# Placing and loading the modulation tiles of a two-layer transformer chain between its dense weight tiles

## The reference, cut to what matters

```
cond_lat = jax.nn.silu(c)
cond_ctx = jax.nn.silu(c_ctx)
for i in range(DEPTH):
    mod = (cond_lat @ ada_w[i] + ada_b[i])[:, None, :]
    modc = (cond_ctx @ ada_w[i] + ada_b[i])[None, None, :]
    sh1, sc1, g1, sh2, sc2, g2 = jnp.split(mod, 6, axis=-1)
    ...
    h = modulate(rmsnorm(x, norm1_g[i]), sh1, sc1)
```

## Time and profile before

| | us |
|---|---|
| median of three runs | 2321.1 |
| profiled execution, its own time | 2323.7 |
| its span in the profile | 2321.9 |
| TensorE busy | 1981.4 (85%) |
| GpSimd busy | 1005.7 (43%) |
| VectorE / ScalarE busy | 760.8 / 736.1 |
| mean TensorE clock, share of full | 0.924 |

### The profile page before, as it was taken

How to read it: one execution, slowest core, us unless ns; L and a number is a source line. 1 busy time by engine, 2 the same in 40 slices (tenths; PEclk the granted TensorE clock), 3 DMA queues, 4 the chain that set the end, 5 groups by cost and what they waited for, 6 DMA issues and landing times. The chain is left out here.

```text
span 2321.9 us, 29302 instructions
## 1 busy us (share of the span) xinstructions
PE 1981.4 (85%) x11525; PEld 1490.7 (64%) x11525; DVE 760.8 (33%) x1392; ACT 736.1 (32%) x1024; POOL 1005.7 (43%) x784
## 2 busy tenths in 40 slices
PE   7779878999678886999969897789996998887998
PEld 5456554444346763444448586489986997756997
DVE  3453132111432123111154846841243113453112
ACT  3332221000232330100044544544443444444442
POOL 6226400000344630000066185059885888405896
PEclk9779898999889997999989798899998999998999
DMA  7636748999877657999963053036553665303662
GB/s 256 186 81 205 215 121 346 409 409 409 284 209 225 182 147 243 368 409 409 409 210 127 20 190 108 20 100 191 181 172 108 191 182 186 114 23 104 190 188 91
DMA packets 296005, 477.04 MB, mean 205 GB/s; under 512 B 17786, under 2 KB 197996, under 8 KB 295756
## 3 DMA queue, kind: packets, MB, share of 16 engines
q1 hardware_dynamic: 289260, 458.63, 59.4%
q10 hardware_dynamic: 6624, 16.73, 2.2%
HBM read 474.15 MB, written 1.15 MB: 205 GB/s over the span
## 5 line engine op out<-in xcount | busy, mean ns | idle before, releaser
L604 POOL TENSOR_TENSOR w_lo<-raw,w_hi 128x512 fp32r<-128x512 f32 x780 | 1005.5, 1324 | 1298.0 <-ACT w_hi L1344 1297.9
L668 PE MATMUL PS<-at_hi,w_hi 128*128 128x256 f32 x1680 | 490.2, 292 | 29.6 <-DVE at_lo L1852 15.7
L669 PE MATMUL PS<-at_lo,w_hi 128*128 128x256 f32 x1680 | 483.1, 288 | 0.0
L670 PE MATMUL PS<-at_hi,w_lo 128*128 128x256 f32 x1680 | 482.8, 287 | 0.0
L1344 ACT ACTIVATE w_hi<-raw 128x2048 fp32r<-128x2048 f32 x195 | 371.7, 1909 | 345.7 <-PE PS L670 339.2
L668 PEld LDWEIGHTS PS<-at_hi,w_hi 128*128 128x128 f32 x1680 | 331.0, 197 | 42.2 <-issue 17.0
L669 PEld LDWEIGHTS PS<-at_lo,w_hi 128*128 128x128 f32 x1680 | 330.8, 197 | 3.6 <-issue 2.6
L670 PEld LDWEIGHTS PS<-at_hi,w_lo 128*128 128x128 f32 x1680 | 330.3, 197 | 0.0
L668 PE MATMUL PS<-w_hi,at_hi 128*128 128x512 f32 (+1 forms) x480 | 190.6, 397 | 29.5 <-POOL w_lo L604 7.1
L669 PE MATMUL PS<-w_lo,at_hi 128*128 128x512 f32 (+1 forms) x480 | 187.5, 391 | 0.0
L670 PE MATMUL PS<-w_hi,at_lo 128*128 128x512 f32 (+1 forms) x480 | 186.6, 389 | 0.0
(11 more groups left out here) (298 smaller groups left out, 2364.7 us busy)
## 6 DMA issues: line engine op xcount, KB each, us to landing
raw<-ffn_w_gu SPq DMA_DIRECT2D x132, 512.0 KB, 4.9
raw<-ada_w SPq DMA_DIRECT2D x128, 384.0 KB, 6.2
raw<-l_e_gate SPq DMA_DIRECT2D x80, 512.0 KB, 11.3
raw<-ffn_w_down SPq DMA_DIRECT2D x66, 512.0 KB, 4.0
raw<-l_e_up SPq DMA_DIRECT2D x64, 512.0 KB, 8.4
raw<-l_e_down SPq DMA_DIRECT2D x48, 512.0 KB, 13.7
raw<-diff_w_in SPq DMA_DIRECT2D x48, 512.0 KB, 4.6
H<-l_e_down SPq DMA_DIRECT2D x40, 512.0 KB, 12.7
```

The lines of the kernel that those rows point to most:

```text
L604: ins = nc.gpsimd.tensor_tensor(w_lo[:, n % RING, part], raw[:, order_of(n) % RAW, part], w_hi[:, n % RING, part].bitcast(F32), ALU.subtract)
L668: pe.matmul(dst, s_hi, m_hi, start=first, stop=False)
L669: pe.matmul(dst, s_hi, m_lo, start=False, stop=False)
L670: return pe.matmul(dst, s_lo, m_hi, start=False, stop=last)
```

## The change

The table of counts before each dense tile is now derived from a table of uses, `ADA_USED[n]`: how many modulation tiles TensorE has used before it starts dense tile n. `tile_wait` calls `mods(ADA_USED[n])` itself, so single modulation tiles stand between dense ones. SP loads them so that those used before tile n come ahead of the load of tile n+3. The calls by hand leave at most three in one place where TensorE waits for other engines (four, at the entry of the second layer's experts). SP loads a modulation tile in one transfer of 128 partitions; the semaphore of a slot thus rises by 16 for it and by 32 for a dense tile, and `landed(s)` counts what is due.

```diff
-ADA_BEFORE = ([0] * 9 + [2, 8, 8, 8, 8] + [16] * 8 + [21] * 4 + [26]
-              + [32, 32, 32, 34, 34, 34, 34, 37, 43, 43, 43, 43] + [46] * 8 + [50] * 4 + [55] + [MODS])
+ADA_USED = ([0, 0, 0, 0, 0, 1, 2] + [6, 7, 8, 9] + [14, 15, 15, 16, 16, 17, 17, 18] + [21, 22, 22, 23] + [27, 27, 28, 28]
+            + [32, 32, 33, 34, 36] + [39, 40, 41, 42] + [45, 46, 47, 47, 48, 48, 49, 50] + [53, 53, 54, 54] + [58, 58, 59, 59])
+ADA_BEFORE = [0, 0, 0] + [MOD_TILES if n + 3 in (27, 28, 29) else used for n, used in enumerate(ADA_USED[:-3])] + [MODS]
...
+def landed(s):
+
+    kinds = [kind for kind, _ in SEQUENCE[s % RAW:s + 1:RAW]]
+    later = max(0, s - len(SEQUENCE) + RAW) // RAW
+    return 32 * (kinds.count("dense") + later) + 16 * kinds.count("ada")
...
-                    for half in (slice(0, 64), slice(64, P)):
-                        sp.dma_start(raw[half, s % RAW, 0:MOD_COLS], rows[i, half, :]).then_inc(raw_landed[s % RAW], 16)
+                    sp.dma_start(raw[:, s % RAW, 0:MOD_COLS], rows[i]).then_inc(raw_landed[s % RAW], 16)
...
             def tile_wait():
+                if c.get("tile") < MOE_AT[1]:
+                    mods(ADA_USED[c.get("tile")])
                 pe.wait_ge(lo_done, c.lo(c.get("tile")))
...
-                mods((18, 48)[layer])
+                mods((20, 52)[layer])
                 to_at(X, wait=False)
-                mods((21, 50)[layer])
+                mods((21, 53)[layer])
...
-                attention(8, 1, scores, lambda i: 2, pv, lambda it: mods((21, 50)[layer] + min(it + 1, 5)))
+                attention(8, 1, scores, lambda i: 2, pv, lambda it: mods((23, 54)[layer] + min((it + 1) // 2, 4)))
...
             def moe(layer):
-                mods(MOD_TILES * layer + 28)
+                mods(MOD_TILES * layer + 31)
...
                     gemm(1)
-                    mods(2)
                     gemm(1, 256)
-                    mods(6)
+                    mods(5)
...
                     def fill(it):
+                        if it < 12:
+                            mods(6 + (it + 1) // 4)
...
-                    mods(16)
+                    mods(14)
                     at_wait()
...
                     tile_end(ins)
-                    mods(43)
+                    mods(39)
                     at_wait()
```

More of the change, by code:

```diff
@@ L635, in mods @@
                     s = ADA_AT[a]
-                    pe.wait_ge(raw_landed[s % RAW], 32 * (s // RAW + 1))
+                    pe.wait_ge(raw_landed[s % RAW], landed(s))
                     for n in range(3):
@@ L950, in cross @@
                     to_at(H, wait=False)
-                    mods(46)
+                    mods(45)
                     at_wait()
@@ L1240, in _ @@
                     to_at(mem_rows, wait=False)
-                    mods(8)
+                    mods(6)
                     at_wait()
@@ L1245, in _ @@
                     pe.wait_ge(fill_freed, 4)
-                    mods(12)
+                    mods(11)
                     for t in range(NT):
-                        mods(12 + t)
+                        mods(11 + t)
                         transpose_src()
@@ L1264, in _ @@
                     gemm(1)
-                    mods(34)
+                    mods(33)
                     to_at(HL, wait=False)
                     gemm(1)
-                    mods(36)
                     transpose_src()
@@ L1277, in _ @@
                         ins.then_inc(wb_full, 1)
-                    mods(37)
+                    mods(36)
                     at_wait()
@@ L1338, in split @@
                 s = order_of(n)
-                use = 32 * (s // RAW + 1)
+                use = landed(s)
                 act.wait_ge(raw_landed[s % RAW], use if i is None else i * (32 * LOOP_TILES // RAW) + use)
```

## The result

The changed kernel takes 2280.53 us (median of four runs, 2272.89 to 2283.97), beside 2318.14 us for the kernel before in the same series (2314.33 to 2323.04). The ratio is 0.9833, with a 95% interval of 0.9806 to 0.986: 37.6 us faster, where 45.7 were forecast. The forecast time was 2275 us with a range of 2258 to 2300.

The account below looks back on a forecast made before the run. It took TensorE's 64.2 us of waits for modulation tiles, loaded in 64-partition halves, as the bound before the DMA-bound experts. Layers of -22.9 and -27.8 gave -50.7, net -45.7 after allowance: 2275 us, range 2258 to 2300.

Parts of the forecast that it names:

- Rival 1: Modulation tile transfers: row length, not half tiles, sets the rate; awaited tiles land 1.6 us later, 2290 us; chance 0.13.
- allowance of 5.0: Ten places where a single tile lands within 2 us of its use, half a microsecond each: +5.0 us.
- cross attention: Both layers: a wait of 3.17 us and 0.85 us of half clock go, -4.0 us each.
- Behind the pooling tile: Second layer: three tiles fit below VectorE's evacuation, 5.4 us remain of 26.1: -20.7 us.
- Entry of the experts: Remaining modulation tiles before the experts stop holding up TensorE: -4.0 us in the first layer, -12.0 in the second.
- A landing time of 4 us: Whole modulation tile on an idle queue: 1.92 us of transfer and 2 to 3 us of latency.
- number 39: Second layer's `w_out`: single modulation tile queued on SP behind dense tile 35, a new wait of +6.2 us.
- the first batch: End of the input projection, first layer: three tiles stand first, ending at 73; 14.2 us for 26.0, -11.7.
- The fourth single wait of the first layer: `w_out` and values: the fourth single tile waits for its load behind a layer norm on ScalarE, +1.8 us.
- Rival 2: TensorE stands still less, so its clock gives 10 us more, with no waits at single tiles: 2262 us; chance 0.15.
- a change of this distance: Sign against the argument: distances from the experts' start to the end, after 930 us, should stay the same.
- Rival 3: Waits move between dense tiles: 17 single tiles at 4.2 us, 71 us in all, 2334 us; chance 0.10.

Follow-up runs that it names:

- e3: Kernel before, each modulation tile still in two transfers but cut by columns, each reaching 128 partitions with 3072-byte rows: 2292.41 us, ratio 0.9894.
- e5: The change, with the experts' tiles loaded in transfers of 64 partitions, four of 256 KB instead of two of 512 KB: 2641.81 us, one run.
- e2: Kernel before with its old order, each modulation tile loaded in one transfer of 128 partitions: 2290.04 us, ratio 0.9874.
- e7: The change itself, unaltered, measured again: 2278.03 us, ratio 0.9829.
- e4: The change, with modulation tile 39 used one dense tile later and the order of loads kept: 2277.35 us, ratio 0.9824.
- e8: The change, with the four modulation tiles inside each cross attention used after every head instead of every second: 2291.53 us, ratio 0.9882.
- e1: The change's order and uses, with modulation tiles loaded in two halves of 64 partitions as before: 2303.33 us, ratio 0.9938.
- e6: The change, order of loads kept, with the modulation tiles it waits for used one or two places later: 2265.13 us, ratio 0.9789.

## Why the prediction was right, and where its terms were off

**The mechanism.** The partitions that a transfer reaches set the rate, as the prediction took it. Rival 1 (0.13, the row length) falls by e3 and e5, and by e2, which moves whole tiles with rows of 6144 bytes at 396 GB/s. For the estimate of 1.92 us of transfer for a whole tile that is 1.99. The Trainium skill's "DMA: Bandwidth & Descriptors", "Where 436 GB/s comes from", would have memory bind near 358 GB/s, or 2.2 us a tile: the experts' 409 GB/s and e2's 396 speak against it on this one core, and the measurement decides.

**The sum** was 50.7 us before an allowance of 5.0; 41.8 had come by the second layer's experts. That it came so near is in part luck: cross attention paid 9.3 us more than forecast, and the other rows together 18 us less, of which the allowance covers 5. (One small slip of the sum: 26.0 less 14.2 is 11.8 and not 11.7.) Its terms, as the table shows them:
- *Exact.* Behind the pooling tile, -20.7 for -20.7: the waiting tiles went under the evacuation. Entry of the experts, -12.0 forecast and -11.6 measured, and -4.0 and -3.6 in the first layer. The attention's +1.0 for +1.0 is a coincidence: in e7 and e4 the row would read -1.2 and -1.8.
- *A landing time of 4 us, taken for an idle queue.* This is the step that was mis-sized. The 4 us are right for a tile that finds the queue empty: 4.2 from issue to use for the one issued at 66.65 and used at 70.87, and for the one of 216.09. They don't hold behind another load: 6.3 for the one issued at 67.04 right behind it, 6.8 for number 39, 7.2 for the one used at 245.15, and 7.9 for tile 2, issued at 60.97 right behind dense tile 9 and used at 68.90; the median is 5.2. In the first batch the sum had even less, 3.5 us from the slot to the landing at 70. That makes most of the step from -11.7 to -8.8, since the batch ended at 75.2 and not at 73, and number 39's wait 8.34 and not 6.2.
- *A slot that came free late.* The fourth single wait of the first layer was 3.29 and not 1.8 us, but its tile landed after 4.2 us as estimated. It was issued late: its slot had to wait for GpSimd, which was behind the layer norm. The sum had seen this wait and made it too short. GpSimd, then SP:

```profile
213.53 2.54 POOL L611 TENSOR_TENSOR w_lo<-raw,w_hi 128x512 fp32r<-128x512 f32 x2
216.09 0.34 SPq L431 DMA_DIRECT2D raw<-ada_w  x1
```

- *Half clock behind such a wait.* The walk had priced only the wait. The dense tiles behind the waits of 3.29 and 8.34 us took 7.8 and 7.1 us and not 5.5, so 2.3 and 1.6 us more. With the longer wait that makes most of the step from +8.1 to +12.3 at `w_out` of the second layer.
- *Waits not seen at all.* 3.06 us at 245.15 inside `xq` (+4.5 there, with a forecast of +2.9 for `xq` and `xo` together), 1.5 to 2.1 us at three places of the second layer's keys and values (+3.8 for +0.3), and 1.67 us for VectorE ahead of the pooling tile, where -1.4 became +0.3. Six waits for modulation tiles that the sum had not named come to 9.6 us, against the allowance of ten places with half a us each: fewer places, and each of them dearer. Three of the six, 6 us of them, are tiles queued right behind a dense tile.
- *Cross attention paid twice the forecast.* -8.1 and -9.2 for -4.0 each. The prediction counted the wait of 3.17 us and the half clock behind it, and put nothing down for the tiles themselves. In the kernel before, four of them stand ahead of the first product with `V`, in the change two: that product comes 15.9 us after the stage's first product before and 8.7 after in the first layer, 16.4 and 7.7 in the second. e8, with four again, loses 13.5 us over both layers. This is the largest gain that was missed, and it pays for about half of what the other rows lost.

**The other rivals.** Rival 2 (the clock gives more, 2262 us) didn't come: much of the half clock work went with the batches, but some came back behind the single tiles' waits. In the two profiled executions the unchanged part behind the experts' start of the second layer got shorter too, 1392.3 to 1383.3 us, with the clock's share a little higher (each row: length, busy times, clock, DMA share, GB/s; before, then after):

```profile
926.00:2320.00 1394.00, 1235.22 (x7648) 1004.26 (x7647) 489.74 (x808) 521.54 (x710) 738.32 (x572) 0.94 0.53 178
```

```profile
885.00:2270.00 1385.00, 1228.03 (x7640) 999.96 (x7639) 495.34 (x808) 521.78 (x710) 739.42 (x572) 0.95 0.53 180
```

Nothing there is changed. The prediction had named a change of this distance as a sign against its argument, so it has to be looked at. In the six traces with the new order (the change, e1, e4, e6, e7, e8) the part takes 1383.3 to 1390.3 us, 1388.8 in e7, and in the three with the old order (before, e2, e3) 1392.4. Part of it is the spread from run to run; whether a small gain of the change is in it isn't settled. The medians don't need it: 37.6 us, and 38.5 in e7, are less than the 41.8 and 40.1 that the experts' start had moved, so they and not the two traces measure the change. Rival 3 (waits of 3.5 us at 17 places, slower) had its mechanism right and its frequency wrong. Single tiles did hold up dense products, at no more than eight places (eleven waits, less the three of the first batch), and e6 wins 12.9 us by moving such uses; the price never came near the point at which the change would lose.

## What to carry to other kernels

Give every transfer all 128 partitions, and cut by columns if it has to be cut. A small load issued right behind a large one lands late: price it from the trace by what is ahead of it (4.2 us alone, 6.8 to 7.9 behind 1 MB here), and place its use behind the next dense tile, not ahead of it, together with the uses that follow if their loads are as late (e4 moved one and won nothing, e6 moved seven). Work slipped into a stage that passes from head to head costs its full length ahead of the first head's last product, and more if it has to wait. Behind it, it costs next to nothing where TensorE waits for a head's softmax anyway, so put it there.

## What was not expected of the hardware

The page's busy share of the DMA engines doesn't tell a slow transfer from a fast one: 1.04 at 222 GB/s (e5) and 1.03 at 409, so the GB/s beside it has to be read with it. And a wait between dense tiles costs more than itself: 8.34 us of standing still were followed by 1.6 us more at half clock, and 3.29 us by 2.3 more.
